# Taking the constant-table products out from in front of TensorE's waits, in a two-layer hybrid decoder step

## What is computed

```
h  = rmsnorm(x);  z = h @ w_in
a  = MLA attention (6 heads; prompt rows, and sample rows over a paged past of 2048)
b  = dilated window attention (6 heads, three patterns), prompt and sample
c  = silu(layernorm(depthwise conv(GLU(z))))
x += concat(a, b, c) @ w_out
h  = rmsnorm(x);  q = h @ peer_wq;  two-stage top-16 of 128 x 128 experts, 8 heads
x += sum over the chosen experts of  gate * gelu(h . u[e]) * v[e]
```

## Time and profile before

| | |
|---|---|
| median of 3 runs | 2450.76 us |
| lowest, highest | 2450.35, 2460.01 us |
| the profiled execution | 2454.91 us |
| its span, first to last instruction | 2453.0 us |
| busy: PE, PE weight loads, DVE, ACT | 97%, 83%, 66%, 53% of the span |
| chain that ended last | PE 93%, DVE 3% |
| mean granted TensorE clock | 0.993 |

### The profile page before, as it was taken

One profiled execution on the slowest core, in us unless ns is written; L12 is line 12 of the kernel. 1 busy time (PEld: TensorE's weight loads), 2 busy tenths in 40 slices (PEclk: granted clock), 3 DMA queues, 4 the chain that ended last, 5 costly groups with the idle time before them and its releaser, 6 DMA issues.

```text
span 2453.0 us, 46266 instructions
## 1 busy us (share of the span) xinstructions
PE 2386.6 (97%) x17270; PEld 2039.9 (83%) x17270; DVE 1613.6 (66%) x3839; ACT 1302.9 (53%) x2891; POOL 102.5 (4%) x140
## 2 busy tenths in 40 slices
PE   6999999999999999999999899999999999999998
PEld 3565689999999988778866557899999999887786
DVE  2376267786677777667734742776857778776776
ACT  1344234546776666666614432345467766666665
POOL 2100010000000000000021000100000000000000
PEclk9999999999999999999999999999999999999999
DMA  7441337776656567676564314477766665676664
GB/s 247 150 143 71 120 125 261 252 255 234 218 197 220 199 215 242 221 236 205 172 206 139 121 70 155 153 260 250 262 220 215 200 220 200 224 231 217 196 191 153
DMA packets 143628, 482.35 MB, mean 197 GB/s; under 512 B 25730, under 2 KB 52672, under 8 KB 139310
## 3 DMA queue, kind: packets, MB, share of 16 engines
q1 hardware_dynamic: 132926, 439.11, 53.4%
q0 software_dynamic: 10496, 40.42, 4.6%
HBM read 476.20 MB, written 104.21 MB: 237 GB/s over the span
## 4 chain that ended last, share of the span: by engine, by line
PE 93%; DVE 3%; SPq 2%; DMA 1%; issue 1%; ACT 0%; DVEq 0%; ACTq 0%
PE ps L1090 30%; PE ps L1136 28%; PE ps L801 12%; PE ps L1080 6%; PE ps L1102 5%; PE ps L766 3%; PE ps L1065 1%; PE ps L791 1%; PE ps L810 1%; DVE big L1639 1%; PE ps L926 1%; PE ps L929 1%; PE ps L942 1%; PE ps L956 0%; PE ps L887 0%
## 5 line engine op out<-in xcount | busy, mean ns | idle before, releaser
L1090 PE MATMUL ps<-parts_hw,parts_uv 128*128 128x256 f32 x6144 | 797.2, 286 | 1.0 <-DVE parts_uv L1985 1.0
L1090 PEld LDWEIGHTS ps<-parts_hw,parts_uv 128*128 128x128 f32 x6144 | 751.5, 191 | 1.9 <-issue 1.6
L1136 PE MATMUL ps<-parts_uv,parts_hw 128*128 128x512 f32 x3072 | 703.3, 391 | 10.5 <-DVE parts_uv L2014 5.7
L1136 PEld LDWEIGHTS ps<-parts_uv,parts_hw 128*128 128x128 f32 x3072 | 577.7, 188 | 138.3 <-issue 11.9
L2014 DVE TENSOR_TENSOR parts_uv<-region,parts_uv 128x512 fp32r<-128x512 f32 x512 | 351.8, 692 | 189.0 <-ACT parts_uv L1385 164.0
L1385 ACT CAST parts_uv<-region 128x512 fp32r<-128x512 f32 x512 | 317.4, 621 | 244.9 <-PE ps L1136 243.9
L1985 DVE TENSOR_TENSOR parts_uv<-ps,parts_uv 128x512 fp32r<-128x512 f32 x512 | 329.2, 685 | 127.5 <-ACT parts_uv L1367 124.9
L1367 ACT CAST parts_uv<-ps 128x512 fp32r<-128x512 f32 x512 | 285.4, 614 | 1.3 <-PE ps L1080 1.3
L1404 ACT ACTIVATE big<-ps 128x256 f32<-128x256 f32 (+26 forms) x256 | 131.6, 514 | 243.0 <-PE ps L1090 242.9
L1080 PE MATMUL ps<-identR,rows_r 128*128 128x128 f32 x2048 | 202.3, 242 | 1.4 <-ACT big L1358 1.4
L1080 PEld LDWEIGHTS ps<-identR,rows_r 128*128 128x128 f32 x2048 | 191.7, 139 | 1.7 <-ACT big L1358 1.7
(11 more groups left out here) (289 smaller groups left out, 2049.6 us busy)
## 6 DMA issues: line engine op xcount, KB each, us to landing
region<-in_peer_u SPq DMA_DIRECT2D x256, 512.0 KB, 4.0
region<-in_peer_v SPq DMA_DIRECT2D x256, 512.0 KB, 4.2
out<-in_state_win_k SPq DMA_DIRECT2D x16, 1536.0 KB, 9.3
out<-in_state_win_v SPq DMA_DIRECT2D x16, 1536.0 KB, 8.2
out<-in_state_win_k SPq DMA_DIRECT2D x16, 1534.5 KB, 9.3
out<-in_state_win_v SPq DMA_DIRECT2D x16, 1534.5 KB, 7.3
region<-in_peer_wq SPq DMA_DIRECT2D x8, 2048.0 KB, 8.4
big<-in_state_win_k SPq DMA_DIRECT2D x48, 192.0 KB
```

The lines of the kernel that those rows point to most:

```text
L1090: mm = pe.matmul(ps[:, 4 + j % 2, 0:SEQ], uT[j % 2][a][:, 128 * c:128 * c + 128], hp[b][:, c, :], start=(c == 0 and n == 0), stop=(c == KD ...
L1136: mm = pe.matmul(ps[:, 2 * half + t, :], wp[j % UN][a][:, 128 * t:128 * t + 128], vp[j % 2][b][:, 512 * half:512 * half + 512], start=(j = ...
```

## The change

All products of the constant tables are taken out, with the helper: 46 products of 128x512 and 8 of 128x128 over the two layers. No wait is added or removed except the second, equal `begin` in `keep_busy`; in front of `turn_probs(u)` the bank is now waited for after `exp_ready` or `cnt_ready`, not before. No other engine's stream changes.

```diff
                 for done, rows in ((2, (0, 2)), (3, (1,))):
-                    if first and done == 3:
-                        for i in range(4):
-                            pe.matmul(bank(name, 0)[:, T:T + P], ident[:, :], iota[:, :], start=True, stop=True)
-                    elif now[0] and not first and done == 2:
-                        keep_busy((name, 5), 4)
                     pe.wait_ge(hn_ready[now[0]], first + done)
...
-            def keep_busy(name, n):
-
-                o = begin(*name)
-                for i in range(n):
-                    pe.matmul(o[:, 0:512].rearrange("p (a b) -> p a b", a=4), ident[:, :], iota[:, :].unsqueeze(1).to_broadcast([P, 4, P]), start=True, stop=True)
...
-                keep_busy(("qbT", 0), 2)
                 pe.wait_ge(qk_ready, 1)
...
                 def turn_probs(u):
-                    if u >= 5:
-                        keep_busy(("PT", u), 2)
                     if u < NH:
                         pe.wait_ge(exp_ready, u + 1)
...
-                keep_busy(("yt", 0), 2)
                 pe.wait_ge(y_ready, 1)
...
-                keep_busy(("ycT", 0), 3)
                 pe.wait_ge(ln_ready, 3)
```

## The result

| | before | after |
|---|---|---|
| median (lowest to highest), 5 runs each | 2452.64 us (2450.35 to 2460.01) | 2479.78 us (2472.28 to 2485.61) |
| the profiled execution | 2454.91 us | 2485.61 us |
| its span | 2453.0 us | 2483.8 us |
| mean granted TensorE clock | 0.993 | 0.971 |

The changed kernel is slower: the ratio is 1.0095, interval 1.0076 to 1.0114. On the 2450.76 us that the prediction started from, that is 2474 us: inside the range of 2443 to 2477, but 18 us above the forecast of 2456, outside the likeliest case's own range of 2448 to 2463, and in the region of rival 2. The outcome that I held likeliest, "same" within half a per cent, missed too: the difference is nearly twice that. The range holds the result only because its upper end reaches into rival 2.

A forecast was written before the change was run, and what follows sets the result against it. PE was taken to bound the kernel, busy 97% of the span with 93% of the chain. Gains of 12.2 us against clock costs of 17.6 us gave +5.4 on 2450.8: 2456 us, range 2443 to 2477.

The forecast's parts named there:

- likeliest case: Whole kernel: "same" within half a per cent, own range 2448 to 2463 us, centre 2456, chance 0.50.
- rival 2: Attention, 195 to 236 us and its twin: clock once down stays low until the output projection; 2472 us, chance 0.31.
- `qk_ready`: First transposes behind this wait could start 1.8 us sooner, but the third group waits for VectorE's copy; nothing gained.
- the output projection: Its start, after PE keeps only six transposes from 236.4 to 243.6 us: cost 2.4 us per layer, 4.8 in all.
- the attention: From step 7 on, new waits bring three more low-clock stretches per layer: cost 4.9 us each layer, 9.8 for both.
- u = 5: Attention step 5, at 171.86 us: exponential already ended, PE could go on at once; gain 1.7 us per layer.
- "fT": Third row block, L776 at 278.78 us: four products of 128x128 take 1.0 us; gain 0.7 us per layer.
- u = 7, 8 and 11: Attention steps whose counts ended before PE's work started: gains of 1.3, 1.7 and 0.7 us per layer.
- u = 6: Attention step 6: PE already idle 1.32 us after its products; no gain, the wait grows to 3.1 us.
- The start of layer 2: PE idle 4.2 us from 1230.8 to 1235.0, then restarts on a low clock: cost 3.0 us.
- The bound of 3.65 us: Highest price of one dense restart, from the same work cold in layer 1 against layer 2.
- The sweeps: Both sweeps of each layer, 340 to 1231 us and its twin: the same to within a microsecond.

The follow-up runs named there:

- The put-back: The changed kernel with the two products of 128x512 ahead of `qk_ready` put back, nothing else: 2471.48 us, ratio 1.0059.
- The run with more products: The kernel before with one more product of 128x512 ahead of `q_ready` and two ahead of `wsel_ready`: 2461.72 us, ratio 1.0010.
- the second set: One of three sets of experiments, each with its own runs of the kernel before; the changed kernel, run again beside it, took 2479.26 us.
- the convolution put back: The changed kernel with the products ahead of `y_ready` (2) and `ln_ready` (3) put back, nothing else: 2471.93 us, ratio 1.0072.

## Why the prediction was right in direction and too small in size

The gains and the mechanism, a clock that falls where the products were, held. The costs, 17.6 us in the sum, were 42.9: `qk_ready` stood at nothing, the output projection was too low by a factor of three, the attention by 4.6 us. That the time still lies in the range is owed to rival 2, not to the sum.

**The gains were there.** u = 5: ahead of it the lag was 2.1 us, and at the past's scores of step 6 it was 0.4 (174.00 before, 174.36 after): the 1.7 us arrived. "fT": +12.7 to +12.0 us, and +29.8 to +29.1: 0.7 each time, as counted. At u = 7, 8 and 11 the lag went from +3.9 to +2.7, from +4.3 to +2.6 and from +4.1 to +3.4 us, near the 1.3, 1.7 and 0.7 of the list. That the gain of u = 5 didn't last is something that I had not seen: PE waits longer at u = 6, because VectorE itself now waits for a window of keys that is still being loaded (VectorE's timeline after, then the load's issue, before and after, then PE's waits after).

```profile
179.37 0.95 DVE L1635 TENSOR_TENSOR big<-big,ps 128x768 f32<-128x768 f32 x1 [2.13 <-DMA big<-in_state_win_k]
```

```profile
171.29 1.39 SPq L563 DMA_DIRECT2D big<-in_state_win_k  x3
```

```profile
174.30 1.38 SPq L563 DMA_DIRECT2D big<-in_state_win_k  x3
```

```profile
185.29 0.90 PE L766 MATMUL ps<-ident,region 128*128 128x128 f32 x3 [5.43 <-DVE den L1728]
...
197.76 0.55 PE L766 MATMUL ps<-ident,region 128*128 128x128 f32 x3 [3.40 <-DVE den L1728]
```

I had forecast 3.1 us of idle time at u = 6 and about 3.3 ahead of u = 7: 5.43 and 3.40. "No DMA waits for these products" was true, and beside the point. VectorE reached that place at about the time of before (177.2 and 176.8 us); it is the load that was issued 3.0 us later. It stands in the queue behind the loads of values, which wait for the past's mix (`load_vw`): they went out at 170.71 us where before at 167.34, because PE was late and the mix, L928, took 1.93 us at 168.71, inside a low stretch, where it took 1.08 in before. So a fall of the clock came back once more through a load: VectorE's 2.13 us are part of PE's 5.43.

**The start of layer 2** was the term with the best row: 3.0 us taken, 2.7 measured, idle time 4.2 forecast, 4.02 read:

```profile
1248.80 3.94 PE L778 MATMUL ps<-ident,big 128*128 128x128 f32 x24 [4.02 <-DVE big L1493]
```

**`qk_ready`, priced at nothing,** cost 7.7 us. The step that failed is "PE reached that wait at about this moment with the products in front. Nothing." It was right that no time would be gained. It left out what I had applied to the other places: with the products gone PE waits in the midst of small products, 1.83 us here, and the clock was low for ten microseconds from there. The put-back took 0.39% off, about 9.6 us.

**The output projection, 2.4 us per layer,** was mis-sized by a factor of three: 14.7 us in both layers against 4.8. I had looked at the dense products and asked how they would restart. The low clock begins at 232.6, in the thin work ahead of the convolution, and it stays through both waits (2.41 and 3.50 us of idle time) and 4.9 us into the dense products:

```profile
238.85 3.58 PE L999 MATMUL ps<-big 128*128 128x6 f32 x16
...
248.24 1.54 PE L766 MATMUL ps<-ident,big 128*128 128x128 f32 x6 [2.41 <-DVEq L1793]
253.29 1.71 PE L766 MATMUL ps<-ident,big 128*128 128x128 f32 x6 [3.50 <-DVE big L1807]
254.93 16.46 PE L790 MATMUL ps<-region,big 128*128 128x512 f32 x32
```

The bound of 3.65 us came from a restart. It isn't one for a low clock that covers the thin work too. I had made no forecast of these two waits' length beyond the products' own; they grew from 0.50 and 1.34 us by 1.9 and 2.2 us, where the products took 1.8 and 2.7. Of layer 1's 8.6 us, 5.0 came in the thin work up to L1022 (lag +4.1 to +9.1), 1.1 over the two waits, and 2.5 in the dense products (+10.2 to +12.7), which is about what I had priced.

**The attention, 9.8 us,** measured 14.4. The direction and the order of size were right (9.3 us in layer 2 and 5.1 in layer 1, where 3.3 us had come back from the two missing low stretches). But the place was not as rival 2 had it: from 195 to 236 us the clock after was not low throughout.

```profile
195.00:236.00 41.00, 33.43 (x450) 21.85 (x451) 26.40 (x105) 13.52 (x34) 0.00 (x0) 0.88 0.15 53
```

It fell in short pieces and came back each time, as in the likeliest case. **Rival 2** had the right time, 2472 to 2480 us, and the right mechanism, a low clock that stays on in mixed work; its place was behind the attention, not in it. I gave it 0.31 because the sixteen transposes had been fast again at 132.61; that row says that the clock comes back, and nothing on a place with two waits in it. It had not even come back for good "at once": behind the 3.8 us at 0.94 of the earlier trace rows the next sixteen transposes of before were at the lower level again, in work without any of the products. That favoured rival 2, and I had left it out.

```profile
123.50 3.62 PE L766 MATMUL ps<-ident,big 128*128 128x128 f32 x16
```

```profile
124.00:127.00 3.00, 3.00 (x16) 3.00 (x16) 2.93 (x9) 0.00 (x0) 0.00 (x0) 0.51 0.60 192
```

On the Trainium skill's rule in "TensorE: Matmul & The Clock Gate", Part 4, on transposes, the rows stay divided: in the run with `qk_ready` put back, 39 transposes in a row ran at 1.00 for 6.22 us, which speaks against it; in the changed kernel 21 of them filled a low stretch behind a wait of 1.83 us and the clock did not rise in them, which it would explain, but neither did it in the sixteen products of 64x264 behind them (5.87 us), which are no transposes. No run here tells it from small products of another kind.

**The sweeps** were to be the same within a microsecond. They grew by 1.8 and 1.6 us with the PEER stage ahead of them, 3.4 in all, and nearly all of it comes at one place of each layer, in the second sweep: a low stretch right behind a wait for VectorE. First layer 1 and layer 2 after, then the wait in layer 1, after and before.

```profile
1110.00:1113.00 3.00, 3.00 (x8) 2.31 (x7) 2.33 (x5) 0.51 (x1) 0.00 (x0) 0.50 0.59 170
...
2338.60:2342.00 3.40, 3.40 (x9) 2.67 (x9) 2.69 (x6) 0.62 (x1) 0.00 (x0) 0.51 0.56 165
```

```profile
1109.66 10.68 PE L1120 MATMUL ps<-parts_uv,parts_hw 128*128 128x512 f32 x39 [2.88 <-DVE parts_uv L1998]
```

```profile
1097.44 7.77 PE L1136 MATMUL ps<-parts_uv,parts_hw 128*128 128x512 f32 x33 [2.87 <-DVE parts_uv L2014]
```

The wait is as long in before, and there the clock stayed up. The run with more products has both stretches too (1100.4 to 1103.8 us at 0.50, 2315.5 to 2319 us at 0.51), with every product of before in place. So these 3.4 us aren't shown to come from the change: whether the clock falls at this wait differs between executions.

The excess by the table is 7.7 - 0 at `qk_ready`, 9.9 at the output projection, 4.6 in the attention and 3.4 in the sweeps, less 0.3: 25.3 us, the 42.9 that it cost less the 17.6 that I had. In medians, where the two kernels differ by 27.1 us and not by 30.7, it is a little less. So most of the excess is in two terms, the one put at nothing and the one mis-sized.

## What to carry to other kernels

A product that nobody reads isn't waste by itself: count what it takes from the path and, beside it, the places at which the clock would fall without it, and price these with the whole work up to the next dense stage, thin work and waits included, not with one restart. Such products were wide here (512 columns); narrow ones (4 columns) of the same duration made this kernel 1.8% slower, and with half of the wide ones no difference from the whole number could be told (1.0012 [0.9994, 1.0031]). A removed product that seems to free time ahead of another engine's copy here only moved the wait into the middle of the work behind it.

## What the runs showed of the hardware that I had not expected

- A PE that is busy all the time doesn't keep its clock: 50.00 of 50 us busy at a granted clock of 0.73 with narrow products (240 to 290 us), 10.20 of 10.20 us at 0.50 in the changed kernel (106.3 to 116.5 us).
- Products of 64 rows and 4 columns took 62 ns each back to back (2.96 us for 48), and those of L1002 37 ns (0.89 us for 24). Which of the differences between them makes it wasn't tried.
- One kernel's executions spread by what the clock does. Beside the second set the fastest of before, 2448.6 us, had 0.995, the slowest, 2463.8 us, 0.986: 15.2 us for 2 x 0.009 x 2456 = 44 us of low time, 0.34 us each, near the 0.39 from the comparison of the two kernels. With the convolution put back it was 2460.1 us at 0.983 and 2481.8 at 0.974.
